# Folding a per-group map and a scale into the rows of the output matrix, in a streaming encoder layer

## The reference, cut to what matters

```python
h = x @ w_in                                   # q | k | v | u, 512 columns each
a_out = _stick_breaking(q, k_all, v_all, start_pos)
diffs.append((hi - lo) / cnt - ue[:, P:, lo_c:hi_c])          # for each of 4 groups
d = jnp.stack(diffs, axis=2)
y = jnp.einsum('btgc,gcd->btgd', d, pool_w).reshape(B, T, C)
p_out = y * pool_scale
mix = jnp.concatenate([a_out, p_out], axis=-1) @ w_out        # w_out (1024, 1024)
x1 = _layer_norm(ALPHA * x + mix, ln1_g, ln1_b)
y = _layer_norm(ALPHA * x1 + (silu(x1 @ w_gate) * (x1 @ w_up)) @ w_down, ln2_g, ln2_b)
```

## Time and profile before

| | us |
|---|---|
| median of 3 executions | 2588.72 (2587.19 to 2590.2) |
| span of the profiled execution, first to last instruction | 2585.7 |
| TensorE busy | 2521.1 (98%) |
| weight loads busy | 2147.9 (83%) |
| VectorE, ScalarE, GpSimd busy | 1574.1, 1154.3, 1172.3 |
| DMA queue of SP | 372.02 MB, 45.7% of 16 engines' time |

### The profile page before, as it was taken

One profiled execution on the slowest core, in us unless ns is written; L12 is line 12 of the kernel. 1 busy time (PEld: TensorE's weight loads), 2 busy tenths in 40 slices (PEclk: granted clock), 3 DMA queues, 4 the chain that ended last, 5 costly groups with the idle time before them and its releaser, 6 DMA issues.

```text
span 2585.7 us, 37584 instructions
## 1 busy us (share of the span) xinstructions
PE 2521.1 (98%) x13894; PEld 2147.9 (83%) x13894; DVE 1574.1 (61%) x2125; ACT 1154.3 (45%) x1932; POOL 1172.3 (45%) x1028
## 2 busy tenths in 40 slices
PE   9999999999999999999999999999999999999998
PEld 9978798787878888878788877878878897999997
DVE  3266336666444357787744477787775345867676
ACT  4465326665232135566531265656654213343333
POOL 4465437755223135456631174556653213354434
PEclk9999999999999999999999999999999999999999
DMA  7697956764446243444254244333532612333232
GB/s 231 193 281 249 355 169 194 225 216 125 136 134 236 82 115 106 127 118 112 89 207 139 98 117 124 103 110 103 147 103 96 223 60 90 96 98 114 91 94 88
DMA packets 211158, 374.43 MB, mean 145 GB/s; under 512 B 30784, under 2 KB 105152, under 8 KB 208928
## 3 DMA queue, kind: packets, MB, share of 16 engines
q1 hardware_dynamic: 210976, 372.02, 45.7%
HBM read 303.86 MB, written 68.09 MB: 144 GB/s over the span
## 4 chain that ended last, share of the span: by engine, by line
PE 82%; DVE 7%; issue 4%; ACT 3%; POOL 2%; DMA 2%; SPq 1%; DVEq 0%; POOLq 0%; ACTq 0%
PE bank L1290 26%; PE bank L1352 19%; PE bank L1240 8%; PE bank L1194 7%; PE bank L1298 7%; PE bank L1092 5%; PE bank L1139 4%; PE bank L1108 4%; DVE left L1922 1%; DMA gw_lo_raw<-in_w_in_dram 1%; DVE acc L1960 1%; POOL gw_lo L2592 1%; PE bank L1217 1%; ACT beta L1476 1%; DVE stats L1942 0%
## 5 line engine op out<-in xcount | busy, mean ns | idle before, releaser
L1290 PE MATMUL bank<-x1T,gw_hi 128*128 128x512 f32 (+1 forms) x2336 | 712.2, 388 | 3.7 <-DVE hT_lo_raw L2036 2.3
L2522 POOL TENSOR_TENSOR beta<-beta,left 128x512 f32<-128x512 f32 (+2 forms) x326 | 352.5, 1082 | 349.7 <-DVE left L1922 349.2
L1290 PEld LDWEIGHTS bank<-x1T,gw_hi 128*128 128x128 f32 x2336 | 418.8, 188 | 83.7 <-issue 3.2
L1290 PE MATMUL bank<-x1T,gw_lo 128*128 128x512 f32 (+1 forms) x1168 | 447.9, 383 | 0.0
L2549 POOL TENSOR_TENSOR gw_lo<-gw_lo_raw,gw_hi 128x1024 fp32r<-128x1024 f32 x70 | 181.7, 2596 | 424.1 <-ACT gw_hi L1544 423.9
L1467 ACT ACTIVATE aT<-bank 128x512 fp32r<-128x512 f32 (+2 forms) x326 | 173.6, 533 | 427.4 <-PE bank L1108 376.0
L1240 PE MATMUL bank<-x1T,gw_hi 128*128 128x256 f32 (+2 forms) x1472 | 354.6, 333 | 6.3 <-DVE gw_lo L2231 2.5
L2217 DVE TENSOR_TENSOR acc<-bank,acc 128x512 f32<-128x512 f32 x312 | 213.3, 686 | 214.1 <-PE bank L1352 210.6
L1907 DVE TENSOR_TENSOR aT<-bank,aT 128x512 fp32r<-128x512 f32 (+2 forms) x326 | 196.9, 604 | 197.6 <-ACT aT L1467 196.3
L1352 PE MATMUL bank<-dw_hi,hT_hi 128*128 128x512 f32 x728 | 295.6, 406 | 9.8 <-issue 5.7
L1352 PE MATMUL bank<-dw_lo,hT_hi 128*128 128x512 f32 x728 | 287.0, 394 | 0.0
(11 more groups left out here) (223 smaller groups left out, 4709.3 us busy)
## 6 DMA issues: line engine op xcount, KB each, us to landing
gw_lo_raw<-in_w_gate_dram SPq DMA_DIRECT2D x88, 512.0 KB, 3.7
gw_lo_raw<-in_w_up_dram SPq DMA_DIRECT2D x88, 512.0 KB, 3.8
dw_lo_raw<-in_w_down_dram SPq DMA_DIRECT2D x86, 512.0 KB, 4.4
gw_lo_raw<-in_w_in_dram SPq DMA_DIRECT2D x64, 512.0 KB, 4.5
k_st<-kT_scratch SPq DMA_DIRECT2D x160, 128.0 KB, 4.1
v_st<-v_scratch SPq DMA_DIRECT2D x80, 256.0 KB, 4.2
q_st<-qT_scratch SPq DMA_DIRECT2D x128, 128.0 KB, 3.9
wo_raw<-in_w_out_dram SPq DMA_DIRECT2D x16, 1024.0 KB, 5.7
```

Source lines behind the costliest of these rows:

```text
L1290: m = pe.matmul(gu_bank(g, n)[:, 0:w], gw[L % 4][a][:, k, :], x1T[x][:, k, first:first + w], start=k == 0 and s == 0, stop=k == KD - 1 and ...
L2522: pool.tensor_tensor(x[:, 0:w], x[:, 0:w], left[n % RL][:, 1:w + 1], ALU.mult).then_inc(a_done, 1)
```

## The change

`pool_w` (transposed on the host) and `pool_scale` are multiplied into the lower 512 rows of `w_out` on the chip, once: for each group g, `pw` (the scaled map, split into parts) times the 128 rows of `w_out` of that group. The new matrix goes to a scratch in device memory, `wop_d`, and the mix reads its lower half from there. The pooled difference `d` itself is stored to `mixT_scratch`. So:

- `pool_product`, `pool_hi` and `pool_lo` are gone from all 16 u chunks; `store_pooled` moves from slot S+9 to S+6 and stores the parts of `d`; `differences_hi` waits for the store of the previous `d` (`d_stored`) and no longer for `pooled`.
- Four times in block 0, at slots 12, 24, 36 and 48 (`WOP_AT`): SP loads 512 KB of `w_out` six slots earlier; ScalarE rounds them (slot +0), GpSimd splits (+1), TensorE makes six matmuls of 512 columns into banks 3 and 7 (+4), ScalarE and VectorE move half each (+5), SP stores 512 KB (+6).
- ScalarE and VectorE scale and split `pw` at slots 6 and 7.
- Every load of a `w_out` chunk is two DMAs of 512 KB, one from `w_out` and one from the scratch.
- Keys and queries take the two buffers `qk` in turn (`pair_of`). The first attention waits for the four stores too.

```diff
     def pair_of(n):
-        b, kind, c = place(n)
-        return 0 if kind == POOLED else 1 if kind == KEY else 1 - c % 2
+        return place(n)[2] % 2
...
+    WOP_AT = [12, 24, 36, 48]
+    WOP_BANKS = [3, 7]
...
             def load_wo(b, c):
...
-                sp.dma_start(wo[c % 2][2][:], w_out[c])\
-                  .then_inc(wo_loaded[c % 2], 16)
+                sp.dma_start(wo[c % 2][2][:, 0:KD // 2, :], w_out[c]).then_inc(wo_loaded[c % 2], 16)
+                sp.dma_start(wo[c % 2][2][:, KD // 2:KD, :], wop_d[c]).then_inc(wo_loaded[c % 2], 16)
...
             def store_pooled(n):
-                sp.wait_ge(pooled_lo, order_of(n, POOLED) + 1)
-                store_pair(n, mixT_d, SBW + place(n)[2] * P)
+                b, kind, c = place(n)
+                rows = slice(SBW + c * P, SBW + (c + 1) * P)
+                sp.wait_ge(d_lo_done, order_of(n, POOLED) + 1)
+                for j in range(2):
+                    sp.dma_start(r32(mixT_d[j, rows, b * BW:(b + 1) * BW]), r32(d_parts[b][j][:, 0:BW])).then_inc(d_stored, 16)
+                    if b == 0:
+                        sp.dma_start(r32(mixT_d[j, rows, SEQ:TOK]), r32(d_parts[b][j][:, BW + SEEN:BW + SEEN + DEC]))\
+                          .then_inc(d_stored, 16)
+
+            def load_out_pooled(g):
+                if g:
+                    sp.wait_ge(wop_made, g)
+                sp.dma_start(wop_raw[:], w_out_pooled[g]).then_inc(wop_loaded, 16)
+
+            def store_out_pooled(g):
+                sp.wait_ge(wop_moved, 2 * g + 2)
+                sp.dma_start(wop_d[:, :, g, :].rearrange("c p n -> p c n"), wop[:, :].rearrange("p (c n) -> p c n", c=4))\
+                  .then_inc(wop_stored, 16)
...
-                if S - 9 in done_at and place(done_at[S - 9])[1] == POOLED:
-                    store_pooled(done_at[S - 9])
+                if S - 6 in done_at and place(done_at[S - 6])[1] == POOLED:
+                    store_pooled(done_at[S - 6])
+                if S + 6 in WOP_AT:
+                    load_out_pooled(WOP_AT.index(S + 6))
+                if S - 6 in WOP_AT:
+                    store_out_pooled(WOP_AT.index(S - 6))
...
-            def pool_product(n):
...
+            def out_pooled(g):
+
+                pe.wait_ge(wop_split, g + 1)
+                if g == 0:
+                    pe.wait_ge(pw_lo, 1)
+                else:
+                    pe.wait_ge(wop_moved, 2 * g)
+                for half in range(2):
+                    cols = slice(half * 512, half * 512 + 512)
+                    for x, (weight, part) in enumerate(((0, wop_hi), (0, wop_lo), (1, wop_hi))):
+                        m = pe.matmul(bank[WOP_BANKS[half]][:, :], pw[weight][:, g, :], part[:, cols], start=x == 0, stop=x == 2)
+                m.then_inc(wop_made, 1)
...
-                    if S - 7 in done_at and place(done_at[S - 7])[1] == POOLED:
-                        pool_product(done_at[S - 7])
+                    if S - 4 in WOP_AT:
+                        out_pooled(WOP_AT.index(S - 4))
...
+            def pool_weights_hi():
+                act.wait_ge(pre_loaded[1], 16)
+                act.wait_ge(pre_loaded[2], 16)
+                for g in range(4):
+                    m = act.activation(pw[0][:, g, :], pw_raw[:, g, :], ACT.Copy, scale=pscale[:, g:g + 1])
+                m.then_inc(pw_hi, 1)
+
+            def out_pooled_hi(g):
+                act.wait_ge(wop_loaded, 16 * (g + 1))
+                act.activation(wop_hi[:], wop_raw[:], ACT.Copy).then_inc(wop_rounded, 1)
+
+            def move_out_pooled(g):
+                act.wait_ge(wop_made, g + 1)
+                if g:
+                    act.wait_ge(wop_stored, 16 * g)
+                act.activation(wop[:, 0:512], bank[WOP_BANKS[0]][:, :], ACT.Copy).then_inc(wop_moved, 1)
...
+            def out_pooled_lo(g):
+                pool.wait_ge(wop_rounded, g + 1)
+                pool.tensor_tensor(wop_lo[:], wop_raw[:], r32(wop_hi[:]), ALU.subtract).then_inc(wop_split, 1)
```

108 lines of the change are left out of this document (48 added, 60 removed).

## The result

The changed kernel takes 2595.23 us (median of 8, 2592.04 to 2600.89) against 2589.6 us of the kernel before beside it (8): a ratio of 1.0026, 95% interval 1.0018 to 1.0034. By the ratio, which is taken from all executions, it is slower by 6.7 us (0.0026 x 2589.6; the two medians alone differ by 5.6). The forecast was 2586.1, with a range up to 2592. The profiled execution is the longest of the eight: 2600.89 us, span 2599.1, 13.4 more than the span before. So single times in its trace are those of one execution, 5.7 above the median; sizes are taken from the medians of the runs, the trace shows places.

What follows compares the result with a forecast made beforehand. TensorE, busy 98% of the span, was taken as the bound. Matmuls -15.6, given back +10.2, SP and DMA in block 0 +2.0, SP in attention +0.8 make -2.6 us on 2588.7: 2586.1 us, range 2575 to 2592.

Steps and rivals of the forecast that it cites:

- Matmuls removed and added: On TensorE, pooled products removed save 21.2 us, six matmuls four times in block 0 add 5.6; net -15.6 us.
- Given back in blocks 1 to 3: In blocks 1 to 3, TensorE stops later for other late engines or DMA; 10.2 us of 15.5 lost again.
- the places of 453 and 515: Products in blocks 1 to 3 where TensorE would wait for VectorE's `aT` instead; 2.1 and 2.0 us given back.
- the stop at 298: TensorE's 1.30 us stop for a weight split after a late DMA; expected longer by 2 to 4, 4.0 us given back.
- The kept 5.3: In blocks 1 to 3, five plain products and the first with its wait stay saved: 5.3 us.
- SP and DMA in block 0: In block 0, group transfers and earlier stores of d delay a weight load; +2.0 us, bounds 0 and 5.4.
- 2 us for `gw_lo` near 61: In block 0, a sign: TensorE waits about 2 us for `gw_lo` after the late load of slot 24.
- the 3.5 for the groups' transfers at slot 18: In block 0, the second group load and first store, 1 MB in a full DMA window, take 3.5 us.
- SP in the attention stretches: In blocks 1 to 3, stores of d before weight loads delay SP's loads; charged once, +0.8 us.
- GpSimd's splits: In block 0, four new GpSimd subtractions of 2.4 us beside VectorE; charged nothing, 9.6 us if passed on whole.
- rival 3: Four GpSimd splits in block 0 each hold up VectorE 2.4 us, 9.6 reaching TensorE; +7.0, 2595.7; chance 0.03.
- Rival 2: Slower by SP's queue: stores of d before weight loads in blocks 1 to 3 reach TensorE; +7.1, 2595.8; chance 0.09.

Runs made afterwards that it cites:

- e12: Changed kernel with the stores of d at S+9 and without the four groups (map and scale not applied): 2581.15 us, 0.9979 of the kernel before.
- e1: Changed kernel with the stores of d put back to S+9, behind the weight load, in all blocks: 2588.36 us, 0.9999 of the kernel before.
- e4: Kernel before with one matmul of three left in each pooled product, no store moved: 2587.69 us, 0.9995 of the kernel before.
- e8: Changed kernel with the stores of d at S+6 in block 0 alone, at S+9 in blocks 1 to 3: 2595.12 us, 1.0022.
- e16: Changed kernel with stores of d at S+9, the groups' stores at S+8 and their w_out loads one slot later: 2589.0 us, 0.9998.
- e15: Changed kernel with the stores of d at S+9 and the groups' stores at S+8: 2589.19 us, 0.9997 of the kernel before.
- e9: Changed kernel with the stores of d at S+6 in blocks 1 to 3 alone, at S+9 in block 0: 2590.76 us, 1.0009.
- e6: Changed kernel with the stores of d at S+7, one slot in front of the weight load: 2599.68 us (5 executions), 1.0044.
- e11: Kernel before with block 0's store of the pooled product at S+11, one slot in front of the next weight load: 2588.46 us, 0.9999.
- e13: Changed kernel with the stores of d at S+11 in block 0 and at S+9 in blocks 1 to 3: 2589.56 us, 1.0003.
- e3: Changed kernel without the four groups (map and scale not applied), stores of d still at S+6: 2596.86 us, 1.0026 of the kernel before.
- e17: Changed kernel with block 0's key stores at S+5 in place of S+1, stores of d still at S+6: 2592.65 us, 1.0021.
- e18: Changed kernel with block 0's key stores at S+5 and the stores of d at S+9: 2586.89 us, 0.9995 of the kernel before.
- e10: Changed kernel with block 0's two 32-column stores of d at S+9, the two of 512 columns at S+6: 2594.47 us, 1.002.
- e2: Changed kernel with three unused matmuls of 512 columns put in at S+7 of blocks 1 to 3, behind d: 2597.37 us, 1.0032.

## Why the prediction was wrong

Two terms of the sum were too small: what is kept in blocks 1 to 3 (5.2 us) and what the early stores of d cost (4.2). With only one of them wrong the time would have been some 2591.3 or 2590.3, inside the range; together they put it outside.

- **Matmuls removed and added (-15.6): right.** The groups' 5.6 is borne out by e12 (5.2). For block 0 it says -5.7 + 5.6 = -0.1; with the stores late (e1) chunk 15 ends 0.16 us earlier than before.
- **Given back in blocks 1 to 3 (10.2 of 15.5): the mechanism right, the term too small.** The waits at the places of 453 and 515 grew as it says, and so did those in front of the stop at 298, though not that stop itself. But nothing was kept, so this is one of the two steps that failed: in e1 chunk 63, the last of block 3, ends 0.04 us earlier than before, having been 0.16 earlier at chunk 15. So about 15.4 was given back, 5.2 more. e4 shows the same with no store moved, 32 matmuls for 1 us. The kept 5.3 was counted from places without a wait; the next wait further on took that too. Part of it is the clock, which the prediction put at nothing without a word: e1's trace has 17.1 us at 1.2 GHz, e4's 20.5, before has 10.2, and the means of all executions (0.9955 and 0.9961 against 0.9972) allow up to 4.4 and 2.9 us of matmul time for it. No run has these waits without this clock, so how the 5.2 divides between them is not shown.
- **SP and DMA in block 0 (+2.0): the step whose mechanism failed.** It priced the stores of d as bytes in front of one load, the one of slot 24: 1.9 us, less slack. That load was late (issued 48.33 and not 46.84, waited for 6.09), but the wait that the prediction made of it, 2 us for `gw_lo` near 61, is absent. It came out as 1.59 us at 68.35, by way of GpSimd and VectorE, and as a late SP: the largest delays were at slots 36 and 48, where SP issued the load 6.2 and 4.9 us after its buffer was free. The prediction counted SP's issues, and its wait for d, only for blocks 1 to 3. It also stopped at the end of block 0, where the term is nearly right (chunk 15 is 2.7 us later than the -0.1), and didn't follow the lateness into ScalarE's queue, the last queries and the first keys, where it grows to 6.4. By e8 against e1 the stores in block 0 cost 6.0 us. Of the 3.5 for the groups' transfers at slot 18 there is no sign (e16 against e15; e12, within its interval), and 298 GB/s was no ceiling: the same window has 337 after.
- **SP in the attention stretches (+0.8): not shown to be wrong.** e9 is 2.3 us over the kernel before (interval -0.3 to 4.7) and 2.6 over e1.
- **GpSimd's splits: at nothing, nearly right.** TensorE waited 0.64 us for `wop_lo`, once. By e12 the groups cost 5.2 us in all, where their matmuls take 5.6; up to some 3 us more is within the interval, the 9.6 of rival 3 is not.
- **Rival 2 had the sign, the queue and nearly the size** (2595.8), but put it into blocks 1 to 3; by e8 and e9 some seven tenths of it is in block 0. It was given 0.09 because most loads land with slack. In block 0 they don't: in the row at 73.08 of before ScalarE has stood 4.41 us for its load already, so a later issue is passed on to ScalarE.

The sum with the measured terms: -2.6, + 5.2 (nothing kept), + 4.2 (the early stores at 7.0 by e1 and not 2.8) = +6.8; measured +6.7. Both corrections are taken from e1, so that the sum closes is no further evidence.

**Open.** Why stores one slot in front of a load cost at S+7 (e6) and not at S+11 (e11, e13). Why the early stores cost more without the groups (0.0047, 12.2 us, e12 to e3) than with them (0.0027, 7.0 us). The clock would account for it, up to 7.8 us of the one (0.9961 to 0.9931) and up to 2.9 of the other; why it falls so much more is not shown. Why the stores of d cost 0.0026 with the key stores out of the way (e17 to e18), though SP is late by 8.0 us only, and why e6, one slot later than the changed kernel, loses 0.0018 more. In block 0, issues and bytes aren't told apart: e10 halves the issues and the lateness (9.1) and the time moves by less than the interval. That the lateness of SP leads to the late first keys is read from the traces above; no run changed that link alone.

## What to carry to other kernels

A store that becomes ready earlier needn't be issued earlier: on a queue that also carries the loads everything waits for, put it behind the next load. Not every place in front of a load costs (e11, e13), but every place behind one was free here. Price what is moved in such a queue by when each load behind it gets issued, at every load and not at the first, and follow the late one to the next phase. And matmuls removed from an engine that is 98% busy brought next to nothing here, where the next wait took the time back and the clock fell behind longer waits: put cheap work back at these places (e2) and see whether the time moves before counting on them.

## What the runs showed of the hardware

- DMA moved more than the prediction's ceiling from before: 401 GB/s over 45 to 55 us and 402 over 300 to 310, with a share above 1.00, where the earlier trace rows had 298 and 326 for longer stretches (the kernel before has 403 over 300 to 310 as well; that window was not read). A load of 512 KB took 4.5 us from issue to use at 73.00, and 11.8 at 168.67, in a stretch with a share of 1.07. The Trainium skill ("Perfetto Trace Analysis", section "Roofline") gives 358 GB/s as a core's share and some 435 as what its 16 DMA engines can reach when it is alone; the 402 lie above the first and under the second, so the trace agrees.
- Issuing took SP 0.32 to 0.48 us for the stores of block 0 in the rows above, ten of them 4.7 us, as long as the 4.5 us from the issue of the load behind them to its use. The Trainium skill ("DMA: Bandwidth & Descriptors", section "Issuing engines are not separate DMA queues") calls the time to start a DMA usually small against the DMA itself. For one issue that agrees here (0.46 against 4.5); ten in front of one load took as long as the load.
- Right behind waits of 1.67 to 3.32 us the granted clock stood at the lower level for 3.4 us, six times, and once for 6.8; three matmuls of 256 columns took 0.64 us there and 0.35 at 2.4 GHz. Behind waits of 2.16, 1.92 and 2.11 us (at 290.82, 298.60 and 411.10) it did not fall.
- VectorE's operation on 7 elements took 2.23 us beside a split of GpSimd (65.08 us, after), as it did before (2.25) and in e1 (2.24). The length is the same in all three; it cost TensorE 1.59 us only where it came 2.1 us later.
